# Linear attention's transpositions: 32-square blocks turned by VectorE and carried by transfers, in the place of TensorE

## The reference

```python
z = h @ w_in[l]
p, q, k, v, g_lr, r, gate_logits = split_combined(z)
...
o_inter = jnp.einsum('bhik,bhkv->bhiv', qi * jnp.exp(Gi), S)
diff = Gi[:, :, :, None, :] - Gi[:, :, None, :, :]
decay = jnp.exp(jnp.where(mask[:, :, None], diff, -jnp.inf))
A = jnp.einsum('bhik,bhjk,bhijk->bhij', qi, ki, decay)
o_intra = jnp.einsum('bhij,bhjv->bhiv', A, vi)
...
o = rms_norm(o, gla_norm[l]).reshape(B, T, GLA_VALUE_DIM) * jax.nn.silu(r)
y_b = o @ w_branch_b[l]
```

## Time and profile before

| | |
|---|---|
| time, median of 3 runs | 2313.27 us (2313.03 to 2313.41) |
| the profiled execution: its time, its span | 2313.33 us, 2311.5 us |
| PE busy | 2302.2 us, 100% of the span |
| DVE, ACT busy | 1453.9 us (63%), 1173.6 us (51%) |
| TensorE clock granted | 0.999 of full speed |
| DMA queue q1, share of the 16 engines' time | 62.3% |

### The profile page before, as it was taken

The page is one execution under the profiler, slowest core; times in us unless marked ns, Lnnn a source line. Parts: engine busy times, 40 slices in busy tenths (PEclk is TensorE's granted clock), DMA queues, the critical chain, the costliest instruction groups (busy, mean ns, idle before and its releaser), DMA issues.

```text
span 2311.5 us, 27350 instructions
## 1 busy us (share of the span) xinstructions
PE 2302.2 (100%) x10893; PEld 1932.0 (84%) x10893; DVE 1453.9 (63%) x1945; ACT 1173.6 (51%) x1545; POOL 25.6 (1%) x35
## 2 busy tenths in 40 slices
PE   9999999999999999999999999999999999999998
PEld 7888888888888888888888888888888888888887
DVE  6677666656666666676466656685555656565564
ACT  6555645444445744444444444465655456565443
POOL 0000000000000000000000000000000000000000
PEclk9999999999999999999999999999999999999999
DMA  8666655666667566665665666656555665655564
GB/s 294 185 175 173 174 171 172 202 201 203 196 203 271 173 191 196 196 187 197 195 195 191 192 191 218 224 174 192 158 158 162 207 216 151 199 161 153 160 203 136
DMA packets 237839, 438.89 MB, mean 190 GB/s; under 512 B 16688, under 2 KB 42800, under 8 KB 237072
## 3 DMA queue, kind: packets, MB, share of 16 engines
q1 hardware_dynamic: 237280, 436.61, 62.3%
q10 hardware_dynamic: 432, 0.53, 0.1%
HBM read 434.99 MB, written 2.10 MB: 189 GB/s over the span
## 4 chain that ended last, share of the span: by engine, by line
PE 99%; DMA 0%; DVE 0%; ACT 0%; SPq 0%; DVEq 0%; issue 0%; ACTq 0%
PE pm L994 31%; PE pm L996 31%; PE pm L995 30%; PE pb L631 2%; PE pb L832 1%; PE pb L724 1%; PE pb L734 0%; DMA raw<-in_w_in 0%; PE pb L814 0%; PE pb L812 0%; PE pm L989 0%; PE pm L988 0%; PE pm L983 0%; PE pm L987 0%; PE pb L813 0%; PE pm L982 0%
## 5 line engine op out<-in xcount | busy, mean ns | idle before, releaser
L2138 DVE TENSOR_TENSOR wl<-raw,wh 128x1024 fp32r<-128x1024 f32 (+3 forms) x786 | 949.4, 1211 | 731.8 <-ACT wh L1481 729.2
L1481 ACT ACTIVATE wh<-raw 128x1024 fp32r<-128x1024 f32 (+3 forms) x786 | 820.3, 1046 | 923.3 <-PE pm L996 919.0
L994 PE MATMUL pm<-wh,hTh 128*128 128x512 f32 x702 | 276.7, 394 | 0.8 <-DVE wl L2138 0.8
L994 PE MATMUL pm<-wh,x2Th 128*128 128x512 f32 x704 | 273.9, 389 | 0.0
L995 PE MATMUL pm<-wl,x2Th 128*128 128x512 f32 x704 | 273.9, 389 | 0.0
L996 PE MATMUL pm<-wh,x2Tl 128*128 128x512 f32 x704 | 273.9, 389 | 0.0
L996 PE MATMUL pm<-wh,hTl 128*128 128x512 f32 x702 | 273.5, 390 | 0.0
L995 PE MATMUL pm<-wl,hTh 128*128 128x512 f32 x702 | 273.4, 389 | 0.0
L994 PE MATMUL pm<-wh,xT3h 128*128 128x512 f32 (+1 forms) x640 | 250.9, 392 | 0.0
L996 PE MATMUL pm<-wh,xT3l 128*128 128x512 f32 (+1 forms) x640 | 244.9, 383 | 0.0
L995 PE MATMUL pm<-wl,xT3h 128*128 128x512 f32 (+1 forms) x640 | 244.5, 382 | 0.0
(11 more groups left out here) (423 smaller groups left out, 3209.7 us busy)
## 6 DMA issues: line engine op xcount, KB each, us to landing
raw<-in_w_in SPq DMA_DIRECT2D x286, 512.0 KB, 3.7
raw<-in_w_ffn_gate SPq DMA_DIRECT2D x88, 512.0 KB, 4.2
raw<-in_w_ffn_up SPq DMA_DIRECT2D x88, 512.0 KB, 4.1
raw<-in_w_ffn_down SPq DMA_DIRECT2D x88, 512.0 KB, 4.2
raw<-in_w_o SPq DMA_DIRECT2D x64, 512.0 KB, 4.4
raw<-in_w_in SPq DMA_DIRECT2D x68, 256.0 KB, 3.2
raw<-in_w_branch_b SPq DMA_DIRECT2D x32, 512.0 KB, 3.7
raw<-in_w_out SPq DMA_DIRECT2D x32, 512.0 KB, 4.7
```

The costliest lines, as they stand in the source:

```text
L994: e.matmul(o, ah[:, kk, t], h[:, c], start=first, stop=False)
L1481: e.activation(h[:, 0:n], r[:, 0:n], ACT.Copy).then_inc(s["hi"], 1)
L2138: e.tensor_tensor(l[:, 0:n], r[:, 0:n], h[:, 0:n].bitcast(F32), ALU.subtract).then_inc(s["lo"], 1)
```

## The change

The 64 transpositions of PE are gone. In their place DVE turns a whole 128x1024 buffer in one instruction, but only within squares of 32 by 32, into a new buffer `squares` (`sqq` for q and k, `sqo` for o; two new buffers). The squares then have to move between partitions: SP issues 16 transfers for each buffer, each of 32 partitions x 1 KB = 32 KB from SBUF to SBUF, into a third new buffer `across`. ACT and DVE read `across` where they read PSUM before. Per head that is two instructions of DVE and 32 transfers; over four heads 8 and 128. `across` is one buffer for all: q/k of a head and o of the head before it take turns in it, and SP's transfers wait for ACT's or DVE's last read (`qk_c`, `oT_l`).

```diff
+    m.squares = [at("sqq", [128, 4, 4, 2, 32], 8), at("sqo", [128, 4, 4, 2, 32], 214.5)]
+    m.across = at("across", [128, 4, 4, 2, 32], 218.5)
...
+    def across(src, sem, at0, waits):
+        for a in range(4):
+            for r in range(4):
+                if r % 2 == 0:
+                    yield at0 + 2 * a + r // 2
+                for sm, value in waits:
+                    w.wait_ge(s[sm], value)
+                e.dma_start(m.across[32 * r:32 * r + 32, a, :, :, :], src[32 * a:32 * a + 32, r, :, :, :]
+                            ).then_inc(s[sem], 16)
...
+            if n == 0:
+                yield from across(m.squares[0], "d_zq", 72, [("zq", 1), ("la_m", 4)])
             if c == 0:
-                yield 76
+                yield 81
                 w.wait_ge(s["la_d"], 16)
             else:
+                if n == 2:
+                    for h in range(3):
+                        yield from across(m.squares[0], "d_zq", p.end[f"qk{h + 1}"] + 4,
+                                          [("zq", h + 2)] + ([("oT_l", 4 * h)] if h else [("qk_c", 3)]))
+                        yield from across(m.squares[1], "d_zo", p.end[f"v{h}"] + 47, [("zo", h + 1), ("qk_c", 3 * h + 6)])
+                    yield from across(m.squares[1], "d_zo", p.end["v3"] + 34, [("zo", 4), ("oT_l", 12)])
...
-    def qk_turns(h):
-        for i in range(2):
-            yield (p.end[f"qk{h}"] + 8 if h else QK0) + 2 * i
...
-                ins = turn(6 + i, j, blocks[::-1] if i else blocks)
-            ins.then_inc(s["qk_t"], 1)
...
-        for i in range(2):
-            yield at0 + 36 + i
-            free(6 + i)
-            w.wait_ge(s["on_d"], 2 * h + 2)
-            turn_pair(6 + i, m.ring[2 + h % 2], 2 * i).then_inc(s["oT_t"], 1)
-            bank[6 + i] = ("oT_l", 4 * h + 2 * i + 2)
...
+    def high_across(h):
+        for k in range(4):
+            w.wait_ge(s["d_zo"], 256 * h + 256)
+            e.activation(m.oT[h][0][:, k, :].rearrange("p (h a t) -> p h a t", h=2, a=4),
+                         m.across[:, :, k, :, :].rearrange("p a h t -> p h a t"), ACT.Copy, scale=m.gcol("gla", k)
+                         ).then_inc(s["oT_h"], 1)
...
-            for i in range(2):
-                yield (p.end[f"qk{h}"] + 8 if h else QK0) + 1 + 2 * i
...
-                e.activation((m.HQ, m.HK)[i][h][:, :, :, :].rearrange("p h f t -> p f h t"),
-                             view(6 + i).rearrange("p f (h t) -> p f h t", h=2), ACT.Copy).then_inc(s["qk_c"], 1)
+            yield p.end[f"qk{h}"] + 14 if h else QK0 + 11
...
+            w.wait_ge(s["d_zq"], 256 * h + 256)
+            e.activation(m.HQ[h][:, :, :, :].rearrange("p h f (a t) -> p f h a t", a=4),
+                         m.across[:, :, 0:2, :, :].rearrange("p a f h t -> p f h a t"), ACT.Copy).then_inc(s["qk_c"], 1)
+            for half in range(2):
+                e.activation(m.HK[h][:, 1 - half, :, :].rearrange("p f (a t) -> p f a t", a=4),
+                             m.across[:, :, 2:4, half, :].rearrange("p a f t -> p f a t"), ACT.Copy).then_inc(s["qk_c"], 1)
...
                 yield p.end[f"v{h}"] + 7 + n
+                if h and n == 4:
+                    high_across(h - 1)
...
+    def turn_squares(i, src, sem):
+        e.transpose(m.squares[i][:, :, :, :, :].rearrange("p r k h t -> p k h r t"),
+                    src[:, :, :].rearrange("p h (k r c) -> p k h r c", k=4, r=4)).then_inc(s[sem], 1)
+    def low_across(h):
+        w.wait_ge(s["d_gain"], 16)
+        for k in range(4):
+            w.wait_ge(s["oT_h"], 4 * h + k + 1)
+            for half in range(2):
+                hi, lo = (x[:, k, half * 128:half * 128 + 128].rearrange("p (a t) -> p a t", a=4) for x in m.oT[h])
+                ins = e.scalar_tensor_tensor(lo, m.across[:, :, k, half, :], m.gcol("gla", k), hi.bitcast(F32), ALU.mult,
+                                             ALU.subtract)
+            ins.then_inc(s["oT_l"], 1)
...
+    def first_squares(h):
+        yield p.end[f"qk{h}"] + 3 if h else QK0 - 1
+        w.wait_ge(s["ev_a"], p.evac[f"qk{h}"])
+        if h:
+            w.wait_ge(s["d_zq"], 256 * h)
+        turn_squares(0, m.ring[h % 2], "zq")
...
+        if h:
+            yield at0 + 12
+            low_across(h - 1)
```

More of the change, by code:

```diff
@@ L248 @@
 S2_OF = {"ql": 0, "kv": 1, "qm": 0, "uq0": 1, "uq1": 0, "uq2": 0, "uq3": 0, "gc": 0}
-SEMAPHORES = """mm hi lo ev_a ev_d nh sq st_r st_v rstd scl sq0 warm xsq xrd xss msq mrd mss hT_h hT_l pool_m wp_h wp_l dT_h dT paT_h paT_l gu g_h la_m la_d la_a qk_t
-qk_c sc_m g_c sd sc_e e_m lev_m dg v_h at_d a_h av_m on_d oT_t oT_h oT_l sig mix_d mx_r mix_t mix_h mix_l mem_h mem_l rp rp_a xr xt_t
+SEMAPHORES = """mm hi lo ev_a ev_d nh sq st_r st_v rstd scl sq0 warm xsq xrd xss msq mrd mss hT_h hT_l pool_m wp_h wp_l dT_h dT paT_h paT_l gu g_h la_m la_d la_a zq zo d_zq d_zo
+qk_c sc_m g_c sd sc_e e_m lev_m dg v_h at_d a_h av_m on_d oT_h oT_l sig mix_d mx_r mix_t mix_h mix_l mem_h mem_l rp rp_a xr xt_t
 xt_h xt_l mk_t mk_c f_t f_h f_l fs_d sc mx ex rl pt_t pt_c pv ys yt_t y_h y_l ql_t ql_h ql_l kv_t kv_h kv_l kp_t kp_c qm_t
@@ L689, in decay @@
             bank[b] = ("la_d", 3 * i + 1)
-    def qk_turns(h):
-        for i in range(2):
-            yield (p.end[f"qk{h}"] + 8 if h else QK0) + 2 * i
-            free(6 + i)
[L696 to L699, removed]
-                ins = turn(6 + i, j, blocks[::-1] if i else blocks)
-            ins.then_inc(s["qk_t"], 1)
-            bank[6 + i] = ("qk_c", 2 * h + i + 1)
     def head(h):
@@ L915, in background @@
         for h in range(4):
-            yield from qk_turns(h)
             yield from head(h)
@@ L1331, in background @@
             if h >= 2:
-                w.wait_ge(s["qk_t"], 2 * h - 2)
+                w.wait_ge(s["zq"], h - 1)
                 w.wait_ge(s["dg"], 2 * h - 2)
@@ L1339, in background @@
                     e.activation(m.latmp[:, i, :], m.latmp[:, i, :], ACT.Ln, bias=1.0).then_inc(s["la_a"], 1)
[L1340 to L1346 removed]
+            yield p.end[f"qk{h}"] + 14 if h else QK0 + 11
+            w.wait_ge(s["xrd"], 4)
+            w.wait_ge(s["pool_m"], 8)
+            w.wait_ge(s["d_zq"], 256 * h + 256)
[4 more added lines that the diff above has]
+                             m.across[:, :, 2:4, half, :].rearrange("p a f t -> p f a t"), ACT.Copy).then_inc(s["qk_c"], 1)
             yield p.end[f"v{h}"]
@@ L1367, in background @@
             if h >= 2:
-                w.wait_ge(s["oT_t"], 2 * h - 2)
+                w.wait_ge(s["zo"], h - 1)
             taken(0, f"r{h}", m.ring[2 + h % 2], ACT.Silu, "x")
@@ L1378, in background @@
                 squares(m.pb[4 + half][:, :], m.ssq[f"h{h}"][:, half:half + 1])
[L1379 to L1382, removed]
         for c in range(4):
             for br in range(2):
+                if br == 1 and c == 0:
+                    yield p.end["v3"] + 46
+                    high_across(3)
                 yield p.end[f"g{'ab'[br]}{c}"] + 2
@@ L1905, in head @@
                 yield at0 + 13 + n
-            w.wait_ge(s["qk_c"], 2 * h + 2)
+            w.wait_ge(s["qk_c"], 3 * h + 3)
             w.wait_ge(s["sc_e"], 8 * h + n + 1)
@@ L1958, in head @@
                                    ALU.mult, ALU.mult).then_inc(s["on_d"], 1)
-        for i in range(2):
-            yield at0 + 37 + i
-            low_gain(6 + i, m.oT[h], 2 * i, "gla", 2 * i, "oT_h", 4 * h + 2 * i + 2, "oT_l")
+        if h < 3:
+            yield from first_squares(h + 1)
+        yield at0 + (36 if h < 3 else 33)
+        w.wait_ge(s["on_d"], 2 * h + 2)
+        if h:
+            w.wait_ge(s["d_zo"], 256 * h)
+        turn_squares(1, R, "zo")
     def pooled(c):
@@ L1986, in decay @@
             e.scalar_tensor_tensor(tm, lo, -2.0, tm, ALU.mult, ALU.add).then_inc(s["la_d"], 1)
+        yield from first_squares(0)
         for i in range(4):
@@ L2022, in background @@
                 name = f"g{'ab'[br]}{c}"
+                if br == 1 and c == 0:
+                    yield p.end["v3"] + 47
+                    low_across(3)
                 yield p.end[name]
@@ L2026, in background @@
                 w.wait_ge(s[f"d_bi{br}"], 16 * c + 16)
-                w.wait_ge(s["qk_t"], 8)
-                w.wait_ge(s["oT_t"], 8)
+                w.wait_ge(s["d_zq"], 1024)
                 for half in range(2):
```

## The result

The change made the kernel slower: 2332.55 us, median of 4 runs (2327.59 to 2334.54), against 2313.21 us before (2313.03 to 2313.41). The ratio is 1.008, with a 95% interval of 1.0063 to 1.0098, so +19.3 us where 7.2 less were forecast. The profiled execution took 2333.02 us, with a span of 2331.2 us and a mean granted clock of 0.995 (before 0.999).

A forecast was written before the change was run, and what follows sets the result against it. PE was taken to set the pace everywhere, busy 2302.2 of 2311.5 us. 2313.3 - 7.8 (transpositions removed) + 0.6 (wait at place 1) = 2306.1 us; range 2304.9 to 2308.7, chance 0.83.

The forecast's parts named there:

- What is added, and its cover: Work added on DVE, ACT and SP: covered in the sum by idle time; what counts is the order, at three places.
- the line "SP": SP's queue in head 0: a load (0.4), four transfers (1.7), two loads (0.9), last two transfers; last issued about 114.8.
- place 1: Head 0, end of v0: ACT waits for transfers, low part of step 86 late; PE waits 0.6 us (0.3 to 1.2).
- Removed from PE: Attention's 64 transpositions in 16 groups, 0.49 us each by the starts, all on the path: 7.8 us saved.
- the rival with the whole listed duration: Attention's transpositions count their full listed duration, 64 x 272 ns = 17.4 us, giving 2295.9 us; chance 0.03.
- The turns: DVE's 8 turns of 128x1024, a shape not in the trace: 1.25 us taken, between 1.23 and 1.74.
- The landing: SBUF to SBUF transfers of 32 KB: 2.6 us to landing taken, between ends of 2.3 and 3.2.
- The rival "slower": Small transfers queue behind weight loads on one DMA queue; slower by 4.6 us from a landing of 8.1 us; chance 0.04.
- Place 2: Heads 1 to 3, middle of E: eight o products ahead of DVE's q and k products; nothing, at most 0.3 each.
- The end of a head: Two small waits lost, `ring` free after one turn and not PE's groups; nobody waited for that, counted at nothing.
- step 3: Apparently Place 3, the transfers in heads 1 to 3: cost nothing.
- Place 3: Transfers in heads 1 to 3: ACT waits 2 us or so, landing may take 6 us before PE waits; cost nothing.

The follow-up runs named there:

- e5_eight: Changed kernel with 8 transfers of 64 KB for a buffer instead of 16, partition to partition, squares not exchanged (output not the reference's): 2308.03 us, ratio 0.9978.
- e10_gpsimd: As `e12_sixteen_mended`, but each buffer's 16 transfers issued by GpSimd's queue, as soon as the squares are there: 2306.44 us, ratio 0.9971.
- e12_sixteen_mended: Changed kernel, 16 transfers on SP, with o's products moved behind E and ACT's wait for `zo` moved ahead of the evacuation of r: 2314.48 us.
- e9_hbm_early_wait: `e7_hbm_late` with ACT's wait for `zo` moved from the evacuation of r to an item ahead of it: 2305.62 us, ratio 0.9967.
- e7_hbm_late: Changed kernel with five transfers through HBM for a buffer, and o's low and high parts moved from the middle of E to behind it: 2307.16 us.
- see 1: Experiment 1, one half of the change at a time against the kernel before: q and k alone 2318.17 us, o alone 2315.02 us.
- the two halves: The change for q and k only (o transposed by TensorE), 2318.17 us, and for o only (q and k by TensorE), 2315.02 us.
- e11_idle: Kernel before with six stops of PE in the feed-forward block, each until GpSimd has done 1 to 6 tiny operations: 2319.88 us, ratio 1.0028.
- e8_turns_alone: Kernel before, all transpositions kept, with the 8 turns added on DVE, unread and without transfers: 2326.12 us, ratio 1.0054.
- e2_o_only: Changed kernel with q and k given back to TensorE, so only o goes by the new path: 2315.02 us, ratio 1.0008 to the kernel before.
- e13_idle_long: Kernel before with six stops of PE in the feed-forward block, each for 9 to 33 tiny GpSimd operations: 2349.58 us, ratio 1.0155.

## Why the prediction was wrong, by its steps

**The step that failed** is the term for SP's queue in "What is added, and its cover": "SP gets 128 transfers of 32 KB, at 0.4 to 0.5 us of its queue each (two loads take 0.89 to issue)", and with it the line "SP" of place 1. An issue took 0.597 us, and a load beside them 0.58 where two had taken 0.89. At 0.44 four transfers and a load are 2.2 us, less than a slab's 2.72; as measured they are 3.07 to 3.59, more. The price was off by a third, but that third lay across the rate at which PE eats slabs: below it the queue has pauses (`e5_eight`), above it SP falls behind with each slab. Place 1: the last transfer was issued at 117.3 and not at 114.8 (SP began 0.75 us late and needed 1.8 us more), and landed at 119.9 and not at 117.4; PE waited 3.28 us and not 0.6. That this is the cause is shown twice: with half the issues (`e5_eight`, the rest of the order as it was but for the last two issues) or another queue (`e10_gpsimd` against `e12_sixteen_mended`) the wait at v0's end is gone.

The Trainium skill, "DMA: Bandwidth & Descriptors", section "Issuing engines are not separate DMA queues", says that starting transfers from several engines saves only the sequencer's time for starting them, which it calls usually small relative to the transfer itself. Here the first part agrees (the landings of GpSimd's transfers are 3.3 to 3.5 us, no shorter). The second agrees for one transfer, 0.597 us to issue and 2.4 to 2.8 to land, and not for a buffer: 16 issues in a row are 9.6 us, and the move to GpSimd's queue made 8.0.

**Removed from PE**, -7.8 us: right. `e9_hbm_early_wait`, where PE waits nowhere in the attention, gives -7.66. The price by starts, 0.49 for a group, holds (each group's place in the changed kernel gives it back); the rival with the whole listed duration is out.

**The turns**, 1.25 us taken: 1.24 and 1.215, right. **The landing**, 2.6 taken from 2.3 to 3.2: 2.8 and 2.4, right. The rival "slower" had named this as its mechanism, with a landing of 8.1 us or more; the time came out on its side, but by the issue ahead of the landing. I gave the queue's length to the path of one buffer and never set its rate against that of the slabs.

**Place 2**, "Cost: nothing, at most some 0.3 for each": in the changed kernel PE waits 1.74, 3.34 and 2.92 us there. With fewer issues 0.80 and 0.53 us remain, the first of them smaller by 0.27 once the products of o go behind E (`e7_hbm_late`), and 0.53 twice the table load, which I had not looked for: the second wait in front of an activation was counted at nothing in "The end of a head". So the step's own size, at most 0.3 for a head, was right, and what filled the place came from step 3 and from a row of ACT that I had not read.

**Place 3**, the transfers of q and k in heads 1 to 3: ACT waits 7.4, 5.6 and 5.7 us at `hq` where 2 or so were forecast, and PE pays little for it directly, 0.30 us at 195.7. As for o, "The transfers of o have about as much. Cost: nothing": wrong, by the same price and by what it does to DVE and back to SP (see 1). In 6.5, 4.8, 4.0 and 7.4 us ACT did nothing at `high_across`. The first of these led to PE's wait of 2.28 us at 217.4, the first three to the waits before E, and the last to 1.67 and 1.50 us of PE's idle time after the attention, a place that the prediction did not have.

**Not in the prediction:** that a wait costs more than its length. Of the 27 us between the -7.8 and the measured +19.3, 8.2 came from the granted clock. The four runs of the changed kernel fit this: the one of 2327.59 us has a mean clock of 0.998, the others, of 2332.08 to 2334.54, 0.995 or 0.996.

**What stays open:** why the waits of the two halves together are so much longer than alone was read from the timelines, not tested; what makes an issue of 32 KB take 0.6 us is not shown; the same 16 transfers due in one row on SP were not tried, so how much of `e10_gpsimd`'s 8.0 us is the queue and how much the order is not divided; 1.3 us of `e11_idle` are not explained; and `e12_sixteen_mended` moves two things at once, so its 18 us are not divided between them. The waits before E need both conditions: they go with fewer issues and the old order (`e5_eight`, but for 0.80 and 0.53 us), and they go with the sixteen issues and the new order (`e12_sixteen_mended`).

## What to carry to other kernels

Where a queue carries the loads that feed the bound engine, set its issues for each period against the period, not only their sum against the span: here 0.6 us for each small transfer, four in 2.72 us, was past the point, and two were free. Give such transfers to a queue with nothing behind them, or make them few and large, even by way of HBM (five transfers and two landings beat sixteen and one). And a forecast that leaves a wait of several microseconds on TensorE should add the time at half clock behind it, and look for what a second wait does to the instruction that gets it.

## What was not expected of the hardware

- An issue on SP's queue costs by the number of transfers far more than by their size: 0.597 us at 32 KB, 0.544 at 64 KB, 0.497 at 128 KB (on 32, 64 and 128 partitions), 0.40 for those that go through HBM. Weight loads between small transfers took 0.58 us, 0.37 where there were pauses.
- The clock does not follow from the length of a wait alone. In `e8_turns_alone` PE idled 2.27 us three times, and half clock came with the third only; 1.89 us was followed by it in `e2_o_only`, 2.52 us in `e13_idle_long` was not. In all these profiles none up to 1.74 us was, and all from 2.92 us on were. The fall can come before PE goes on: at 378.2 us of the changed kernel, where PE waited until 378.9.
- A table load of ACT ran ahead of its activation's wait with one semaphore to wait for, and behind with two (at 277.04 us in `e9_hbm_early_wait`, at 278.21 in `e7_hbm_late`).
